# Conformer convolution in 64x64 quarters of TensorE: 16 token phases, two units at once, fp32 operands that are not split

## What is computed

```python
def conformer_conv(v, gg, dw, dw_b, ln_g, ln_b, pw):
    z = v * jax.nn.sigmoid(gg)
    z = dwconv(z, dw, dw_b, CONF_K // 2, CONF_K // 2)   # 31 taps along the tokens, 256 channels, + dw_b
    mu = jnp.mean(z, axis=-1, keepdims=True)
    var = jnp.mean(jnp.square(z - mu), axis=-1, keepdims=True)
    z = (z - mu) * lax.rsqrt(var + LN_EPS) * ln_g + ln_b
    return jnp.einsum('bnc,ce->bne', jax.nn.silu(z), pw)
```

## Time and profile before

| | us |
|---|---|
| median of 3 runs | 777.88 (775.5 to 778.16) |
| the profiled execution | 776.39 |
| its span, first to last instruction | 774.3 |
| PE busy | 723.8 (93%) |
| DVE busy | 519.9 (67%) |
| ACT busy | 463.4 (60%) |
| POOL busy | 218.4 (28%) |

### The profile page before, as it was taken

The page is one execution under the profiler, slowest core; times in us unless marked ns, Lnnn a source line. Parts: engine busy times, 40 slices in busy tenths (PEclk is TensorE's granted clock), DMA queues, the critical chain, the costliest instruction groups (busy, mean ns, idle before and its releaser), DMA issues.

```text
span 774.3 us, 10037 instructions
## 1 busy us (share of the span) xinstructions
PE 723.8 (93%) x3548; PEld 566.7 (73%) x3548; DVE 519.9 (67%) x807; ACT 463.4 (60%) x756; POOL 218.4 (28%) x262
## 2 busy tenths in 40 slices
PE   3885989999999999999999989799999999999997
PEld 1573767767777778767877767677787888888885
DVE  4377752776899799687995765577746574756422
ACT  4166653599898996897896972333554142534311
POOL 0022334110431254123431055322211244434321
PEclk9698999999999999999999999989999999999999
DMA  9998002444354555345444045345378767867531
GB/s 362 359 322 264 14 36 74 110 110 126 112 164 124 154 160 180 111 133 164 151 147 140 34 157 167 81 125 166 106 247 283 252 212 255 301 199 252 175 131 60
DMA packets 89219, 130.11 MB, mean 168 GB/s; under 512 B 22769, under 2 KB 54129, under 8 KB 87633
## 3 DMA queue, kind: packets, MB, share of 16 engines
q1 hardware_dynamic: 84800, 115.44, 45.5%
q0 software_dynamic: 4368, 14.03, 6.8%
HBM read 91.17 MB, written 38.27 MB: 167 GB/s over the span
## 4 chain that ended last, share of the span: by engine, by line
PE 74%; ACT 7%; DVE 6%; issue 5%; DMA 5%; POOL 2%; SPq 1%; DVEq 0%; ACTq 0%; POOLq 0%
PE bank L1506 23%; PE bank L1508 22%; PE bank L1507 22%; PE bank L1586 4%; DMA wm<-in_w_mod 3%; DVE xg L1160 1%; ACT bank L861 1%; ACT fbuf L878 1%; POOL xTh L604 1%; DVE xTl L1168 1%; ACT Ib L908 1%; PE bank L1542 1%; DMA pv<-scratch_u 1%; DVE xg L1140 1%; PE bank L1634 1%
## 5 line engine op out<-in xcount | busy, mean ns | idle before, releaser
L1506 PE MATMUL bank<-xTh,wh 128*128 128x512 f32 (+1 forms) x592 | 238.5, 403 | 10.4 <-DVE xTl L1168 4.8
L1508 PE MATMUL bank<-xTh,wl 128*128 128x512 f32 (+1 forms) x592 | 230.8, 390 | 0.0
L1507 PE MATMUL bank<-xTl,wh 128*128 128x512 f32 x576 | 226.5, 393 | 0.0
L1506 PEld LDWEIGHTS bank<-xTh,wh 128*128 128x128 f32 x592 | 112.7, 190 | 45.6 <-issue 13.1
L1508 PEld LDWEIGHTS bank<-xTh,wl 128*128 128x128 f32 x592 | 112.4, 190 | 23.6
L1507 PEld LDWEIGHTS bank<-xTl,wh 128*128 128x128 f32 x576 | 109.7, 190 | 21.7 <-issue 1.2
L1506 PE MATMUL bank<-xTh 128*128 128x512 f32 (+1 forms) x272 | 104.2, 383 | 1.7 <-issue 1.1
L1507 PE MATMUL bank<-xTl,xTh 128*128 128x512 f32 x256 | 99.6, 389 | 0.0
L1508 PE MATMUL bank<-xTh,xTl 128*128 128x512 f32 x256 | 99.6, 389 | 0.0
L894 ACT ACTIVATE ustage<-bank 128x512 f32<-128x512 f32 x56 | 32.5, 591 | 77.8 <-PE bank L1508 77.8
L1506 PEld LDWEIGHTS bank<-xTh 128*128 128x128 f32 x272 | 51.1, 188 | 12.1 <-issue 2.3
(11 more groups left out here) (189 smaller groups left out, 1397.4 us busy)
## 6 DMA issues: line engine op xcount, KB each, us to landing
scratch_u<-ustage SPq DMA_DIRECT2D x72, 256.0 KB, 3.6
wraw<-in_w_in SPq DMA_DIRECT2D x18, 512.0 KB, 4.9
wm<-in_w_mod SPq DMA_DIRECT2D x8, 1024.0 KB, 14.4
xg<-in_x SPq DMA_DIRECT2D x16, 512.0 KB, 9.4
yb<-scratch_y SPq DMA_DIRECT2D x32, 256.0 KB, 3.5
gb<-scratch_u SPq DMA_DIRECT2D x32, 256.0 KB, 5.1
xres<-in_x SPq DMA_DIRECT2D x16, 512.0 KB, 4.7
out<-tout SPq DMA_DIRECT2D x15, 512.0 KB, 3.0
```

Of the source, the lines that this page charges most:

```text
L1506: mm(out, wh_, xh_, start=first, stop=False)
L1507: mm(out, wh_, xl_, start=False, stop=False)
L1508: return mm(out, wl_, xh_, start=False, stop=last)
```

## The change

- 16 phases of 128 tokens; a unit handles 8 channels x 16 phases in each of two halves; 3 shifts instead of 5.
- Plain fp32, nothing split: `conv_w_hi`, `conv_w_lo`, `conv_z_hi`, `conv_z_lo` go, with their semaphores.
- `conv_pair` computes two units at once: 2 halves x 3 shifts x 4 quarters = 24 fp32 matmuls of 64x64 on 128 columns into the two units' banks.
- 8 pairs instead of 16 single units, one behind every fourth projection from the 23rd on. Each unit of a pair still has its own bank, its own copy by ACT (256 columns) and its own store.
- Four slots for weights, z and gate instead of 2 and 3. A unit's weights are 192 KB instead of 320 KB; z and gate arrive in runs of 512 B instead of 1 KB.
- The input tiles of the convolution are stored in runs of 32 floats; `load_ln` issues four DMAs instead of two, 4096 runs of 128 B.
- The bias leaves ACT's copy and enters DVE's `ln_sum` and `ln_centre` as the scalar of a SCALAR_TENSOR_TENSOR.
- The host permutes channels within each 16 of the odd units (`conv_order`), since the second unit's halves land on swapped partitions.

The order of units that results, between `gates(q)` and `gates(q + 1)` (P a projection, c a convolution unit):

| q | before | after | | q | before | after |
|---|---|---|---|---|---|---|
| 5 | P c P | P P | | 12 | P c P | P P |
| 6 | P c P P | P c c P P | | 13 | P c P P | P c c P P |
| 7 | c P P | P P | | 14 | c P P | P P |
| 8 | c P P | c c P P | | 15 | c P P | c c P P |
| 9 | c P P c P | P P c c P | | 16 | c P P c P | P P c c P |
| 10 | P c P | P P | | 17 | P c P | P P |
| 11 | P c P | P c c P | | 18 | P c P | P c c P |

The diff, cut to what the text speaks of:

```diff
-PHASES = 8
+PHASES = 16
 NPH = SEQ // PHASES
 GROUP_CH = P // PHASES
-N_CONV = 256 // GROUP_CH
+N_CONV = 256 // (2 * GROUP_CH)
...
-CONV_FROM = 20
-Z_SLOTS = 3
+CONV_FROM = 22
+CONV_SLOTS = 4
 U_SLOTS = 3
...
-        if n >= CONV_FROM and (n - CONV_FROM) % 2 == 0 and convs < N_CONV:
-            units.append(("conv", convs))
-            convs += 1
+        if n >= CONV_FROM and (n - CONV_FROM) % 4 == 0 and convs < N_CONV:
+            units += [("conv", convs), ("conv", convs + 1)]
+            convs += 2
...
-        cwh = a3.take("cvwh", [P, 2, SHIFTS, P], f32r)
-        cwraw = at("cvwraw", [P, 2, SHIFTS, P], a3.off)
-        cwl = a3.take("cvwl", [P, 2, SHIFTS, P], f32r)
-        cg = at("cvg", [P, Z_SLOTS, NPH + 2 * REACH], a3.off)
-        czh = a3.take("cvzh", [P, Z_SLOTS, NPH + 2 * REACH], f32r)
-        cz = at("cvz", [P, Z_SLOTS, NPH + 2 * REACH], a3.off)
-        czl = a3.take("cvzl", [P, Z_SLOTS, NPH + 2 * REACH], f32r)
+        cw = a3.take("cvw", [P, CONV_SLOTS, 2, SHIFTS, P // 2])
+        cg = a3.take("cvg", [P, CONV_SLOTS, 2, NPH])
+        cz = a3.take("cvz", [P, CONV_SLOTS, 2, NPH + 2 * REACH])
...
-                    dst, src = cv_dram[c], ustage[:, U % U_SLOTS, 0:NPH]
+                    dst = cv_dram[2 * c:2 * c + 2].rearrange("h p n -> p h n")
+                    src = phases(ustage[:, U % U_SLOTS, 0:2 * NPH], NPH)
...
+                    src = u_dram[tile, first:first + 2 * GROUP_CH, :].rearrange("(h c) (j n) -> (c j) h n", h=2, n=NPH)
+                    sp.dma_start(dst, src).then_inc(s_cl[b], 16)
...
-            def conv_z_hi(j):
-
-                pool.wait_ge(s_cz, j + 1)
-                mid = slice(REACH, REACH + NPH)
-                round_hi(czh[:, j % Z_SLOTS, mid], cz[:, j % Z_SLOTS, mid]).then_inc(s_czh, 1)
...
-                    src = cv_dram[8 * i:8 * i + 8].rearrange("g (c j) n -> (g c) j n", j=PHASES)
-                    g.dma_start(phases(la[:, i, :], CH // PHASES), src[:, :, part]).then_inc(s_la, 16)
+                    src = cv_dram[N_CONV * i:N_CONV * i + N_CONV].rearrange("g (c j) n -> (g c) j n", j=PHASES)
+                    dst = phases(la[:, i, :], CH // PHASES)
+                    for js in (slice(0, PHASES // 2), slice(PHASES // 2, PHASES)):
+                        g.dma_start(dst[:, js], src[:, js, part]).then_inc(s_la, 16)
...
-                    ins = a.activation(ustage[:, U % U_SLOTS, 0:NPH], pu[U][:, 0:NPH], ACT.Identity,
-                                       bias=par_col("conf_dw_b", c))
+                    ins = a.activation(ustage[:, U % U_SLOTS, 0:2 * NPH], pu[U][:, 0:2 * NPH], ACT.Copy)
...
+                    link(v.tensor_tensor(out=bsum, in0=par_col("conf_dw_b", 0), in1=par_col("conf_dw_b", 1), op=ALU.add))
+                stt(lq[:, 0, :], la[:, 0, :], bsum, la[:, 1, :], ALU.add, ALU.add).then_inc(s_las, 1)
...
-                    v.tensor_tensor(out=lr[:, n % 2, i, :], in0=la[:, i, :], in1=lmu[:], op=ALU.subtract).then_inc(s_zc, 1)
+                    stt(lr[:, n % 2, i, :], la[:, i, :], par_col("conf_dw_b", i), lmu[:], ALU.add, ALU.subtract).then_inc(s_zc, 1)
...
+            def conv_pair(n, c):
+
+                top, low = slice(0, 64), slice(64, 128)
+                for j in (c, c + 1):
+                    pe.wait_ge(s_cwr[j % CONV_SLOTS], 16 * (j // CONV_SLOTS + 1))
+                pe.wait_ge(s_cz, c + 2)
+                pe.wait_ge(s_ev, evacuations_before(N_CU + n + 1))
+                for h in range(2):
+                    for m in range(SHIFTS):
+                        for j in (c, c + 1):
+                            to = (top, low) if j == c else (low, top)
+                            for x, o in zip((top, low), to):
+                                ins = mm(pu[N_CU + n + j - c][o, h * NPH:(h + 1) * NPH], cw[x, j % CONV_SLOTS, h, m, :],
+                                         cz[x, j % CONV_SLOTS, h, m:m + NPH], start=m == 0, stop=m == SHIFTS - 1)
+                            if h == 1 and m == SHIFTS - 1:
+                                ins.then_inc(s_pu, 1)
+
```

More of the change, by code:

```diff
@@ L95, in convs_in_step @@
 def convs_in_step(q, lead):
-    return [g for g in range(N_CONV) if GATES_AFTER[q] <= CONV_AT[g] - lead - (g > 0) < STEP_END[q]]
+    return [g for g in range(N_CONV) if GATES_AFTER[q] <= CONV_AT[g - g % 2] - lead - (g > 1) < STEP_END[q]]
 def mixer_kernel(nc, x, ctx, par, w_mod, b_gate, g_post, w_in, gate_w, pool_w, conv_dw, conf_pw, w_out,
@@ L284, in mixer_kernel @@
         s_czero, s_cgs, s_cz = sem("conf_zeroed"), sem("conf_sigmoid"), sem("conf_glu")
-        s_czh, s_czl = sem("conf_z_hi"), sem("conf_z_lo")
-        s_cl = [sem(f"conf_in{b}") for b in range(Z_SLOTS)]
-        s_cwr, s_cwhi, s_cwlo = [sem(f"convw_in{b}") for b in range(2)], sem("convw_hi"), sem("convw_lo")
+        s_cl = [sem(f"conf_in{b}") for b in range(CONV_SLOTS)]
+        s_cwr = [sem(f"convw_in{b}") for b in range(CONV_SLOTS)]
         s_dve = sem("dve_chain")
@@ L483, in load_conv_w @@
             def load_conv_w(j):
-                if j >= 2:
-                    sp.wait_ge(s_pu, N_CU + CONV_AT[j - 2] + 1)
-                sp.dma_start(cwraw[:, j % 2], conv_dw[j]).then_inc(s_cwr[j % 2], 16)
+                if j >= CONV_SLOTS:
+                    sp.wait_ge(s_pu, N_CU + CONV_AT[j - CONV_SLOTS] + 1)
+                sp.dma_start(cw[:, j % CONV_SLOTS], conv_dw[j]).then_inc(s_cwr[j % CONV_SLOTS], 16)
             def load_conv_z(j):
-                if j < Z_SLOTS:
-                    sp.wait_ge(s_czero, 2)
-                else:
-                    sp.wait_ge(s_pu, N_CU + CONV_AT[j - Z_SLOTS] + 1)
-                half, rows_ = divmod(j, P // GROUP_CH)
-                for tile, dst in ((V_CONF + half, cz), (GG_CONF + half, cg)):
+                b = j % CONV_SLOTS
+                if j < CONV_SLOTS:
+                    sp.wait_ge(s_czero, 1)
+                else:
+                    sp.wait_ge(s_pu, N_CU + CONV_AT[j - CONV_SLOTS] + 1)
+                half, first = divmod(2 * GROUP_CH * j, P)
+                for tile, dst in ((V_CONF + half, cz[:, b, :, REACH:REACH + NPH]), (GG_CONF + half, cg[:, b])):
                     for c in range(NCH):
@@ L745, in _ @@
                     load_pool(0)
-                for j in convs_in_step(q, 4):
-                    conv_z_hi(j)
                 weights_hi(min(STEP_END[q], GATES_AFTER[-1]))
@@ L1325, in weights_lo @@
                     done_w += 1
-                while done_cw < N_CONV and CONV_AT[done_cw] - 4 <= upto:
-                    conv_w_lo(done_cw)
-                    done_cw += 1
             conv(0)
@@ L1341, in _ @@
                 one_minus_a2(q)
-                for j in convs_in_step(q, 4):
-                    conv_z_lo(j)
                 if GATES_AFTER[q] + 1 in WEIGHTS_BEHIND_GATES:
@@ L1401, in ln_sum @@
                     dve.wait_ge(s_pu, N_CU + CONV_AT[-1] + 1)
-                v.tensor_tensor(out=lq[:, 0, :], in0=la[:, 0, :], in1=la[:, 1, :], op=ALU.add).then_inc(s_las, 1)
+                    link(v.tensor_tensor(out=bsum, in0=par_col("conf_dw_b", 0), in1=par_col("conf_dw_b", 1), op=ALU.add))
+                stt(lq[:, 0, :], la[:, 0, :], bsum, la[:, 1, :], ALU.add, ALU.add).then_inc(s_las, 1)
             def ln_square_sum(n):
@@ L1559, in unit @@
                 if o == "conv":
-                    U = N_CU + n
-                    pe.wait_ge(s_cwlo, c + 1)
-                    pe.wait_ge(s_czl, c + 1)
-                    pe.wait_ge(s_ev, evacuations_before(U))
-                    for m in range(SHIFTS):
-                        ins = mm3(pu[U][:, 0:NPH], cwh[:, c % 2, m, :], cwl[:, c % 2, m, :], czh[:, c % Z_SLOTS, m:m + NPH],
-                                  czl[:, c % Z_SLOTS, m:m + NPH], m == 0, m == SHIFTS - 1)
-                    ins.then_inc(s_pu, 1)
+                    if c % 2 == 0:
+                        conv_pair(n, c)
                     return
@@ L1719, in banded @@
     import numpy as np
-    out = np.zeros((N_CONV, GROUP_CH, PHASES, SHIFTS, GROUP_CH, PHASES), w.dtype)
-    grouped = w.reshape(CONF_K, N_CONV, GROUP_CH)
+    half = GROUP_CH // 2
+    out = np.zeros((N_CONV, GROUP_CH, PHASES, 2, SHIFTS, half, PHASES), w.dtype)
+    grouped = w.reshape(CONF_K, N_CONV, 2, GROUP_CH)
     for m in range(SHIFTS):
@@ L1727, in banded, with conv_order @@
                     for c in range(GROUP_CH):
-                        out[:, c, j, m, c, i] = grouped[k, :, c]
-    return out.reshape(N_CONV, P, SHIFTS, P)
+                        out[:, c, j, :, m, c % half, i] = grouped[k, :, :, c]
+    return out.reshape(N_CONV, P, 2, SHIFTS, P // 2)
+def conv_order(v):
+    rows = v.reshape((N_CONV, 2, 2, GROUP_CH // 2) + v.shape[1:]).copy()
+    rows[1::2] = rows[1::2, :, ::-1]
+    return rows.reshape(v.shape)
 def kernel(**inputs):
```

56 lines of the change are left out of this document (17 added, 39 removed).

## The result

The changed kernel takes 800.15 us (median, 799.3 to 802.38), the kernel before 777.86 us on the same chip; the ratio is 1.0305, 95% interval 1.0274 to 1.0336. The forecast was 785.5 us, the range 770 to 796: the direction was right, the size was not, and the time lies outside the range.

The account below looks back on a forecast made before the run. PE was taken to bound the convolution stretch, with ACT 30.3 us behind and its waits limiting any gain; 776.4 us + 1.5 (stretch) + 7.5 (LayerNorm loads) = 785.4, forecast 785.5 us, range 770 to 796.

Parts of the forecast that it names:

- PE's work: Convolution on PE: a pair takes 1.65 us, eight pairs 13.2 us against 28.2 before, so 15.0 us less.
- That it is worth next to nothing: Convolution stretch: of ACT's 25 us waiting for PE, 16 become new waits; the walk gives 240.3 us against 240.6.
- The rival in which the gain passes through: Stretch: ACT not held by slots and banks, -15 us there, 767 to 769 us in all; chance 0.16.
- Slots: ACT's fourth copies wait for the first one's store, 2.3 us in six steps, 0.9 in two: 16 us.
- the very queue that the prediction counted at nothing: SP's loads of z and weights behind the stores, issued two pairs ahead: covered by copies and sigmoids, no cost.
- The prediction's own sensitivity: ACT's walk of the stretch: store landings of 3.5 us add 0.7 us, of 4.5 (unit 3.0) add 5.3 us.
- no slot wait at all: -8: ACT's walk of the stretch: without any wait for staging slots the result changes by -8 us.
- Banks and clock: Stretch: PE waits for banks in steps 6, 9, 13, 16; two of three waits lower its clock, +3.3 us.
- DVE and POOL's relief: Stretch: 32 instructions fewer on each engine shorten ACT's other small waits, -1.5 us, bounds 0 and -11.6.
- The LN loads: Tail: four issues take POOL 3.7 us instead of 1.85, delays reaching 5.55 + 2x by the third: +7.5 us.
- x: Tail: extra time until `la` is complete with 4096 short runs over 2048; taken as 1 us, bounds 0 and 2.6.
- The bias as a scalar: LayerNorm on DVE: costs nothing, as the operation has the same elements and operands.

Follow-up runs that it names:

- run 6: The kernel before with one matmul pass instead of three in the 16 conv units, low-half products left out: 773.1 us, ratio 0.9958.
- run 7: The kernel after with 4352 descriptor bytes, own staging slots for conv units' copies, and every pair's matmuls issued twice: 778.0 us, ratio 1.0019.
- run 4: The kernel after with a staging area of two slots of their own for the conv units' copies: 789.1 us, ratio 1.0171.
- run 1: The kernel after with 4352 instead of 4096 bytes for the descriptors of POOL's DMAs: 785.9 us, ratio 1.0133.
- runs 1 and 3: Besides run 1, the kernel before with each LN load as four DMAs of 512 runs of 256 bytes instead of two of 1024: 779.2 us, ratio 1.0034.

## Why the prediction was wrong, step by step

- **PE's work: right.** A pair takes 1.54 us (at 232.65, 48 records) where 1.65 was taken and 1.3 to 5.1 bounded; 8 x 1.54 = 12.3, so 15.9 us came off where 15.0 was forecast.
- **That it is worth next to nothing: right**, and now shown from both sides: 18.8 us less gave 3.3 (run 6), 10.6 us more cost 3.3 in the median and none of the profiled stretch (run 7), and with the slots' cost gone the stretch is 1.1 us under before's (run 4). The rival in which the gain passes through is out.
- **Slots: right mechanism, mis-sized.** The step took a conv store's landing as 1.7 us from the earlier trace rows. That row is the shortest of sixteen, whose median is 3.0. The 3.0 us for a projection's store is short as well: the 33 of before's stretch have a median of 4.3. (Its subtraction 3.0 - 0.84 gives 2.2 and not 2.3, so its sum is 15 us and not 16.) It also let a store go out with its copy, though loads stand ahead of it on SP, the very queue that the prediction counted at nothing. So fifth copies wait as well: 25.8 us in ten waits instead of 16 in eight. The prediction's own sensitivity is close (landings of 4.5, units 3.0: +5.3 us; measured +4.8 over the forecast stretch, 6.3 against 1.5), and these landings are near the medians that its own trace had. Its "no slot wait at all: -8" was measured as -7.4 (run 4), but from +6.3: its terms without the slots give -6.5 against before, and run 4 has -1.1, so the walk promised more of PE's gain than there was.
- **Banks and clock: right in kind.** PE's bank waits in steps 6, 9, 13 and 16 were forecast at 2.5, 3.2, 4.7 and 1.1 us; the trace has them at 241.09 (1.22), 295.56 (4.12), 361.90 (3.65) and 412.98 (1.93), and two of 1.3 to 1.5 more. Behind 361.90 the clock is 0.50 for 4.1 us, behind 295.56 it is 0.72 over 6 us, and behind the other four waits it stays up; two losses were forecast.
- **DVE and POOL's relief: -1.5 us, not resolved.** No run takes it alone.
- **The LN loads: the step that failed.** "Four issues take 3.7 us, since each has as many runs" looked at what each DMA costs and not at what four of them hold at once. A reserve in which the two of before fitted was overrun by the fourth, and POOL stood 3.8 to 4.1 us more at each of the three loads that the sum priced. The profiled execution's span (798.3 us) missed the forecast one (774.3 + 9.0) by 15.0 us: 14.5 for this, of which the stalls themselves are 11.8, 4.8 for the stretch, where the slots were, less 2.8 for the rest of the tail (4.7 instead of 7.5) and 1.5 ahead of step 5. Without the stall the tail is +4.7 (run 1), where 5.5 was forecast for x = 0.
- **x: wrong, and on the safe side.** DVE never waited for `la` in after, which the prediction had named as a sign of being wrong. From first issue to last landing the four loads took 5.6, 5.9, 8.6 and 6.3 us in before and 5.8, 7.1, 9.2 and 6.8 us in run 1: later by 0.2 to 1.3 us, less than the 1.75 us that the two further issues take, so x came out negative. One DMA of short runs does land later (4.4 us against 3.1, runs 1 and 3), but the four overlap, and each has half the bytes of one of before's two. The estimate of 0.7 us for x that the prediction drew from the Trainium skill (DMA: Bandwidth & Descriptors, Why small descriptors are slow (HBM only)) isn't borne out for the whole load either.
- **The bias as a scalar: nearly nothing.** Each of twelve DVE operations takes 0.75 us or less against 0.69. One thing was missed: the sum of two bias columns, one element wide, stands at 1.23 us in the trace.

```profile
468.81 1.23 DVE L1363 TENSOR_TENSOR sml<-prm 128x1 f32<-128x1 f32 x1
```

- **The range** had no case for a resource that runs out. Its upper end, 796, came from known costs with their bounds; the price of the step from "fits" to "does not fit" was in no row of before, because nothing there stood near the edge.

## What to carry to other kernels

When a change doubles the number of descriptors, staging slots or banks in flight, ask first whether they still fit: such a limit shows no row until it is passed, and then it is paid at every use. An engine at 99% busy is not proof that its work is worth anything: take some of it away in one run, and see what the next engine allows. And before moving work to an idle engine, look at who waits in the queues for it: the same 16 copies on DVE cost 1.1% behind the scans and gave 0.5% ahead of them.
